# Two halves of the activations as one 512-column operand, with both sums added on VectorE

## The reference

```python
def chunk_relpos_attention(h, w_qkv, w_o, rel_bias):      # 16 heads of 64, chunks of 64 tokens
    q, k, v = split_heads(h, w_qkv)                       # h (256 x 1024) @ w_qkv (1024 x 3072)
    ...
        sc = jnp.einsum('bhqd,bhkd->bhqk', q_blk, k[:, :, k0:k1]).astype(jnp.float32) * scale
        sc = sc + bias[None, :, :, BAND - n_keys:]
        p = jax.nn.softmax(sc, axis=-1).astype(v.dtype)
    ...
    return merge_heads(o) @ w_o

def swiglu(h, w_gate, w_up, w_down):                      # 1024 -> 2816 -> 1024
    return (jax.nn.silu(h @ w_gate) * (h @ w_up)) @ w_down

def second_block(x, ...):
    h = rms_norm_2(x, g_pre_mix[i])
    m = chunk_relpos_attention(h, w_qkv[i], w_o[i], rel_bias[i // N_MIXERS])
    x = x + rms_norm_2(m, g_post_mix[i])
    h = rms_norm_2(x, g_pre_ffn[i])
    x = x + rms_norm_2(swiglu(h, w_gate[i], w_up[i], w_down[i]), g_post_ffn[i])
```

## Time and profile before

| | |
|---|---|
| median of 3 runs | 817.92 us (816.59 to 818.11) |
| the profiled execution's own time | 817.35 us |
| its span in the trace | 815.5 us |
| granted TensorE clock, mean | 0.978 of full speed |
| TensorE matmuls busy | 750.4 us (92%), 5438 matmuls |
| weight loads busy | 622.9 us (76%), 5438 |
| VectorE busy | 401.6 us (49%) |
| ScalarE busy | 332.6 us (41%) |
| DMA queue 1 | 67.2% of 16 engines' span |

### The profile page before, as it was taken

How to read it: one execution, slowest core, us unless ns; L and a number is a source line. 1 busy time by engine, 2 the same in 40 slices (tenths; PEclk the granted TensorE clock), 3 DMA queues, 4 the chain that set the end, 5 groups by cost and what they waited for, 6 DMA issues and landing times.

```text
span 815.5 us, 12982 instructions
## 1 busy us (share of the span) xinstructions
PE 750.4 (92%) x5438; PEld 622.9 (76%) x5438; DVE 401.6 (49%) x730; ACT 332.6 (41%) x597; POOL 23.8 (3%) x45
## 2 busy tenths in 40 slices
PE   8989999999999999996866868999998999999996
PEld 7888787888888885552443446999878999999995
DVE  5747755666758531110100108566657655565554
ACT  5476465455444331110110105556546444444442
POOL 1100000000000000000000002100002000000000
PEclk9999999999999999998989989999999999999998
DMA  9637365635987879999999999954343554556101
GB/s 337 208 130 197 138 220 191 221 131 168 380 322 254 344 315 423 420 420 421 420 421 422 420 401 354 364 201 155 121 139 126 184 200 162 194 170 204 53 1 52
DMA packets 83691, 203.99 MB, mean 250 GB/s; under 512 B 6960, under 2 KB 47536, under 8 KB 71088
## 3 DMA queue, kind: packets, MB, share of 16 engines
q1 hardware_dynamic: 83632, 203.15, 67.2%
HBM read 202.09 MB, written 1.05 MB: 249 GB/s over the span
## 4 chain that ended last, share of the span: by engine, by line
PE 77%; DMA 10%; DVE 4%; ACT 3%; issue 2%; SPq 1%; POOL 1%; DVEq 0%; ACTq 0%; POOLq 0%
PE ps L582 57%; DMA ext<-in_w_gate_e 7%; PE ps L863 5%; DMA big<-in_w_up_e 3%; PE ps L884 2%; PE ps L842 2%; PE ps L897 2%; DVE wl L1442 1%; SPq L451 1%; PE ps L945 1%; PE ps L563 1%; ACT junk L1097 1%; PE ps L959 1%; PE ps L973 1%; PE ps L760 1%
## 5 line engine op out<-in xcount | busy, mean ns | idle before, releaser
L1442 DVE TENSOR_TENSOR wl<-raw,wh 128x1024 fp32r<-128x1024 f32 (+3 forms) x180 | 213.5, 1200 | 138.6 <-ACT wh L1088 138.4
L1088 ACT CAST wh<-raw 128x1024 fp32r<-128x1024 f32 (+3 forms) x180 | 183.1, 1031 | 101.3 <-PE ps L582 101.2
L582 PE MATMUL ps<-fra,wh 128*128 128x256 f32 x1168 | 213.7, 285 | 5.9 <-DVE fra L1868 2.6
L582 PEld LDWEIGHTS ps<-fra,wh 128*128 128x128 f32 x1168 | 183.8, 193 | 8.3 <-DVE fra L1868 2.8
L582 PE MATMUL ps<-wh,fra 128*128 128x512 f32 (+3 forms) x668 | 188.8, 368 | 0.7 <-DVE gb L1654 0.4
L582 PE MATMUL ps<-fra,wl 128*128 128x256 f32 x584 | 166.0, 284 | 0.0
L582 PEld LDWEIGHTS ps<-wh,fra 128*128 128x128 f32 x668 | 118.9, 189 | 19.6 <-DVE wl L1442 1.5
L582 PE MATMUL ps<-wl,fra 128*128 128x512 f32 (+3 forms) x334 | 121.3, 363 | 0.0
L582 PEld LDWEIGHTS ps<-fra,wl 128*128 128x128 f32 x584 | 112.7, 193 | 0.0
L863 PE MATMUL ps<-ext,big 128*32 128x256 f32 x480 | 53.8, 446 | 23.0 <-DMA ext<-in_w_up_e 10.7
L582 PE MATMUL ps<-wh,frb 128*128 128x512 f32 x240 | 74.4, 391 | 0.0
(11 more groups left out here) (240 smaller groups left out, 809.8 us busy)
## 6 DMA issues: line engine op xcount, KB each, us to landing
ext<-in_w_up_e SPq DMA_DIRECT2D x23, 1024.0 KB, 26.1
raw<-in_w_in SPq DMA_DIRECT2D x16, 1024.0 KB, 5.1
raw<-in_w_gate_e SPq DMA_DIRECT2D x16, 1024.0 KB, 9.9
raw<-in_w_down_e SPq DMA_DIRECT2D x16, 1024.0 KB, 27.0
raw<-in_w_qkv SPq DMA_DIRECT2D x12, 1024.0 KB, 12.8
raw<-in_w_gate SPq DMA_DIRECT2D x11, 1024.0 KB, 5.2
raw<-in_w_up SPq DMA_DIRECT2D x11, 1024.0 KB, 5.1
raw<-in_w_down SPq DMA_DIRECT2D x11, 1024.0 KB, 4.9
```

The lines of the kernel that those rows point to most:

```text
L582: t = e.matmul(o, a, w, start=first and n == 0, stop=final and n == 2, skip_group_check=not check)
L1088: e.copy(halves(q)[0], piece_view(q)).then_inc(*up("wh", q))
L1442: e.tensor_tensor(l, piece_view(q), h.bitcast(F), ALU.subtract).then_inc(*up("wl", q))
```

## The change

The tile `fra` now holds, for each k, the upper half's 256 tokens and the lower half's 256 side by side, so that `hT_both[:, k]` is one operand of 512 columns. A new function `joint` replaces `features` for queries, keys, gate and up. For each (k, j) it issues one matmul of 512 columns (upper weights by both halves) into a whole bank, and one of 256 columns (lower weights by the upper half) into the left half of that bank. Each j has its own bank, so an output takes two banks. The left half and the right half of a bank are two sums that have to be added: `summed` on VectorE does it with a `tensor_reduce` over the two halves, one per bank, into the place in SBUF where the result goes. Then the scaling works on SBUF in place. The values of a quarter now share one bank, with their matmuls as before. The banks turn with the quarter (`quarter_banks`: queries c and c+1, keys c+2 and c+3, values c+4, modulo 4). Gate always uses banks 4 and 5, up always 6 and 7.

```diff
@@ -274,7 +274,8 @@
         wh, wl, fra, frb = (rounded.enter_context(nc.sbuf_tensor(n, s, FR)) for n, s in (
             ("wh", [P, PIECES, 1024]), ("wl", [P, PIECES, 1024]), ("fra", [P, 8192]), ("frb", [P, 4096])))
     ext = sb("ext", [P, EXT, 2048])
-    hT = [fra[:, a:a + 2048].rearrange("p (t n) -> p t n", t=8) for a in (0, 2048)]
+    hT = [fra[:, 0:4096].rearrange("p (t z n) -> p z t n", t=8, z=2)[:, z] for z in range(2)]
+    hT_both = fra[:, 0:4096].rearrange("p (t m) -> p t m", t=8)
     mT = [fra[:, a:a + 2048].rearrange("p (t n) -> p t n", t=8) for a in (4096, 6144)]
     ym = [frb[:, a:a + 1024].rearrange("p (t n) -> p t n", t=4) for a in (0, 1024)]
     mo = [fra[:, a:a + 2048].rearrange("p (t n) -> p t n", t=8) for a in (0, 2048)]
@@ -428,6 +429,10 @@
         b, half_ = FFN_AT[k]
         return bank[b][:, 256 * half_:256 * half_ + 256]
 
+    def quarter_banks(c):
+
+        return [(c + n) % 4 for n in range(5)]
+
     def causal_parts(s):
         return s[:, 0:128], s[:, 128:384]
 
@@ -630,6 +635,30 @@
                 t.then_inc(*up("piece", q))
                 yield
 
+        def joint(key, banks, freed, ready=(), later=(), row=None):
+
+
+            for q in wt.run[key]:
+                p = wt.pieces[q]
+                h, l = halves(q)
+                for point in ready if p.k0 == 0 else later if p.k0 == 4 else ():
+                    e.wait_ge(*point)
+                e.wait_ge(*at("wl", q))
+                for kk in range(p.rows):
+                    k = p.k0 + kk
+                    if row:
+                        e.wait_ge(*at(*row, k))
+                    for j, b in enumerate(banks):
+                        sl = slice(P * j, P * j + P)
+                        if k == 0:
+                            enter(b, *freed, j)
+                        e.matmul(bank[b][:, :], h[:, kk, sl], hT_both[:, k], start=(k == 0), stop=(k == 7),
+                                 skip_group_check=True)
+                        t = e.matmul(bank[b][:, 0:256], l[:, kk, sl], hT[0][:, k], start=False, stop=(k == 7),
+                                     skip_group_check=True)
+                t.then_inc(*up("piece", q))
+                yield
+
         def attention(name, heads, scores, columns, values):
 
             for step in range(heads + 3):
@@ -924,9 +953,23 @@
         def quarter(c):
 
             first = dict(ready=[at("lo", "pre", 0, 1)], later=[at("lo", "pre", 4, 1)]) if c == 0 else {}
-            yield from features(("q", c), 0, hT, ("kept q", c), **first)
-            yield from features(("k", c), 1, hT, ("kept k", c))
-            yield from tokens(("v", c), 1, hT, ("kept v2", c))
+            yield from joint(("q", c), quarter_banks(c)[0:2], ("summed q", c), **first)
+            yield from joint(("k", c), quarter_banks(c)[2:4], ("summed k", c))
+            b = quarter_banks(c)[4]
+            for q in wt.run["v", c]:
+                p = wt.pieces[q]
+                h, l = halves(q)
+                e.wait_ge(*at("wl", q))
+                if p.k0 == 0:
+                    enter(b, "kept v2", c, 1)
+                for kk in range(p.rows):
+                    for i in range(2):
+                        k, sl = p.k0 + kk, slice(P * i, P * i + P)
+                        t = two_term(bank[b][:, 256 * i:256 * i + 256],
+                                     ((hT[0][:, k, sl], h[:, kk]), (hT[1][:, k, sl], h[:, kk]), (hT[0][:, k, sl], l[:, kk])),
+                                     (k, i) == (0, 0), k == 7, check=False)
+                t.then_inc(*up("piece", q))
+                yield
 
         def other_quarters():
             for c in range(1, 4):
@@ -1034,8 +1077,8 @@
 
         for c in range(12):
             if c < 11:
-                whole(features(("fg", c), 4 + 2 * (c % 2), hT, ("scaled gate", c), row=("lo", "ffn") if c == 0 else None))
-                whole(features(("fu", c), 5 + 2 * (c % 2), hT, ("a", c)))
+                whole(joint(("fg", c), (4, 5), ("summed gate", c), row=("lo", "ffn") if c == 0 else None))
+                whole(joint(("fu", c), (6, 7), ("summed up", c)))
                 if c == 0:
                     spread("ffn row", 2)
             if c:
@@ -1342,7 +1385,8 @@
                 e.wait_ge(*at("piece", last["v", c]))
                 if (c, i) == (0, 0):
                     e.wait_ge(*at("factors"))
-                e.activation(H[:, i, 256 * c:256 * c + 256], bank[2 + i][:, 0:256], ACT.Copy, scale=rr[:, i:i + 1]).then_inc(
+                v = bank[quarter_banks(c)[4]][:, 256 * i:256 * i + 256]
+                e.activation(H[:, i, 256 * c:256 * c + 256], v, ACT.Copy, scale=rr[:, i:i + 1]).then_inc(
                     *up("kept v2", c, i))
 
         def other_quarters():
@@ -1881,23 +1925,38 @@
             e.tensor_copy(krow, bank[b][:, 0:256]).then_inc(*up(name, 0))
             e.wait_ge(*own())
 
+        def summed(name, c, q, dst, banks):
+
+            e.wait_ge(*at("piece", q))
+            for j, b in enumerate(banks):
+                e.tensor_reduce(dst[:, j, :], bank[b][:, :].rearrange("p (z n) -> p n z", z=2), AX, ALU.add).then_inc(
+                    *up("summed " + name, c, j))
+
+        def sum_q(c):
+            summed("q", c, last["q", c], qT[:, 2 * c:2 * c + 2, :], quarter_banks(c)[0:2])
+
+        def sum_k(c):
+            summed("k", c, last["k", c], kT[:, 2 * c:2 * c + 2, :], quarter_banks(c)[2:4])
+
+        rows = krow.unsqueeze(1).to_broadcast([P, 2, 256])
+
         def keep_q(c):
-            e.wait_ge(*at("piece", last["q", c]))
-            e.scalar_tensor_tensor(qT[:, 2 * c:2 * c + 2, :], bank[0][:, :].rearrange("p (j n) -> p j n", j=2), 0.125,
-                                   krow.unsqueeze(1).to_broadcast([P, 2, 256]), ALU.mult, ALU.mult).then_inc(
-                                       *up("kept q", c, 0))
+            v = qT[:, 2 * c:2 * c + 2, :]
+            e.wait_ge(*at("summed q", c, 1))
+            e.scalar_tensor_tensor(v, v, 0.125, rows, ALU.mult, ALU.mult).then_inc(*up("kept q", c, 0))
 
         def keep_k(c):
-            e.wait_ge(*at("piece", last["k", c]))
-            e.tensor_tensor(kT[:, 2 * c:2 * c + 2, :], bank[1][:, :].rearrange("p (j n) -> p j n", j=2),
-                            krow.unsqueeze(1).to_broadcast([P, 2, 256]), ALU.mult).then_inc(*up("kept k", c, 0))
+            v = kT[:, 2 * c:2 * c + 2, :]
+            e.wait_ge(*at("summed k", c, 1))
+            e.tensor_tensor(v, v, rows, ALU.mult).then_inc(*up("kept k", c, 0))
 
         def other_quarters():
             for c in range(1, 4):
                 yield from stream(("q", c))
-                for key, keep in (("k", keep_q), ("v", keep_k)):
+                for key, sums_, keep in (("k", sum_q, keep_q), ("v", sum_k, keep_k)):
                     pieces = stream((key, c))
                     yield next(pieces)
+                    sums_(c)
                     keep(c)
                     yield from pieces
 
@@ -1920,11 +1979,15 @@
             e.wait_ge(*at("factor", "fin", i))
             e.scalar_tensor_tensor(X[:, i, :], MO[:, i, :], rms("fin")[1][:, i:i + 1], gb[:, 1, :], ALU.mult,
                                    ALU.mult).then_inc(*up("block 1", i))
-        whole(stream(("k", 0)))
+        keys_ = stream(("k", 0))
+        next(keys_)
+        sum_q(0)
+        whole(keys_)
         e.wait_ge(*at("factors"))
         spread("krow", rr)
         vals = stream(("v", 0))
         next(vals)
+        sum_k(0)
         spread_row("krow", 6)
         keep_q(0)
         keep_k(0)
@@ -1963,13 +2026,15 @@
                                    ALU.mult, ALU.subtract).then_inc(*up("lo", "ffn", k))
         split_to(wt.run["o", 3][1] + AHEAD)
 
+        def two_of(v):
+            return v.rearrange("p (j n) -> p j n", j=2)
+
         def scaled_gate(c):
             if c:
                 e.wait_ge(*at("al", c - 1))
-            e.wait_ge(*at("piece", last["fg", c]))
-            e.tensor_tensor(S[0].rearrange("p (j n) -> p j n", j=2),
-                            bank[4 + 2 * (c % 2)][:, :].rearrange("p (j n) -> p j n", j=2),
-                            krow.unsqueeze(1).to_broadcast([P, 2, 256]), ALU.mult).then_inc(*up("scaled gate", c, 0))
+            summed("gate", c, last["fg", c], two_of(S[0]), (4, 5))
+            e.wait_ge(*own())
+            e.tensor_tensor(two_of(S[0]), two_of(S[0]), rows, ALU.mult).then_inc(*up("scaled gate", c, 0))
 
         for c in range(12):
             z = c % 2
@@ -1983,9 +2048,10 @@
                     spread("ffn row", rms("ffn")[1])
                     spread_row("ffn row", 2)
                     scaled_gate(c)
-                e.wait_ge(*at("piece", last["fu", c]))
+                summed("up", c, last["fu", c], two_of(S[1]), (6, 7))
+                e.wait_ge(*own())
                 e.wait_ge(*at("silu", c, 0))
-                e.tensor_tensor(S[1], S[0], bank[5 + 2 * z][:, :], ALU.mult).then_inc(*up("a", c, 0))
```

(1 more changed line is left out.)

## The result

The changed kernel takes 820.11 us (median of 8, 819.77 to 821.85) against 818.01 us for the kernel before, measured beside it (median of 8). The ratio is 1.0034, with a 95% interval of 1.0023 to 1.0045: slower, by about 2.8 us by the ratio and 2.1 by the medians. The profiled execution took 820.13 us with a span of 818.4, against 817.35 and 815.5 before.

A forecast was written before the change was run, and what follows sets the result against it. TensorE's own pace was taken as the bound, so savings and new waits count in full: +3.3 (quarters) - 4.5 + 1.7 + 0.1 = +0.6 on 817.35, 817.95; with the median 0.57 higher, 818.5 us, range 814 to 824.5.

The forecast's parts named there:

- likeliest case: Whole kernel: the forecast itself, kept at 0.55, own range 816 to 821, with 0.39 of it within 0.2%.
- the slow reduce: Quarters 1 to 3 and feed-forward start: reduce above 0.69 us; 822 at 0.95 us, 828 at 1.38; chance 0.17.
- the late queue: A late split makes TensorE wait within a piece: 2 to 4 us more, 821 to 823; chance 0.08.
- The reduce: VectorE's sum over a bank's two halves, 60 in all: 0.69 us alone, 1.3 us for a pair.
- Values of quarter 0: They wait for the first reduce to free bank 0: start at 512.85, 0.75 us later than before.
- Keys of quarter 1: Second block waits for bank 0 until quarter 0's values are copied out: starts at 526.9, 1.45 us later.
- Scores: At the ends of quarters 1 to 3, waiting for kept keys: 2.0 us later, then 0.65 more for each, 3.3 finally.
- the forecast wait of 0.95: Quarters 2 and 3: keys kept about 0.95 us after the time the scores used them before.
- Feed-forward: Joining saves 4.5 us; gate 1 waits 1.7 us for reduces between chunks 0 and 1, no other chunk waits.
- forecast saving of 6.1: TensorE, joined matmuls: 12.9 ns for each of 122 quarter and 352 feed-forward pairs, 1.6 + 4.5 us.
- the third rival: Joined matmuls: a pair takes 360 ns as before, the 6.1 us do not come, ends at 824.6; chance 0.07.
- its sign of being right: TensorE's joined matmuls: 512-column and 256-column matmuls 347 ns apart per pair; a pace of 357 ns would show it wrong.

The follow-up runs named there:

- the layout alone: Kernel before with only the two halves placed side by side for each k, matmuls of 256 columns, no reduce: 818.07 us, ratio 1.0003.
- widths in twos: Joint matmuls only in feed-forward chunks from 1 on, ordered two of 512 columns then two of 256; against the kernel before: 814.41 us, ratio 0.9954.

## Why the prediction was right

It forecast 818.5 with 814 to 824.5 and the largest chance, 0.44, on slower; 820.11 came. Its likeliest case was no change, at +0.6 us on the profiled execution, and +2.8 came. The mechanism stands, and the terms are below. The right side was in part luck. Of the 0.44 on slower, 0.32 belonged to three rivals, of which two fell (the slow reduce and the late queue) and the third came by half. And the distance of 1.6 us from the forecast is flattered: the changed kernel's median lies in the early group of its executions and the median before in the late one. Counted from the first matmul of the queries, less the 0.7 behind TensorE's last matmul, the change costs 3.3 us and not 0.6.

- **The reduce**, 0.69 us from two rows at a distance: 0.683 measured. The first rival (a slower reduce) fell with it.
- **Values of quarter 0**: start forecast at 512.85, measured 512.47. The wait was 1.7 us and not 1.1, because TensorE ran this quarter at 1.00 of its clock (0.54 between 499.0 and 502.7 before) and came earlier to the same reduce. Shift of the first scores: +0.44 against 0.75, but counted from the first matmul of the queries +0.91, and +1.74 against the layout alone, whose queries ran at full clock. It costs nothing, since the mask covers it, as forecast.
- **Keys of quarter 1**: wait for `keep_v` to 526.9, measured 526.46 and the start at 526.52.
- **Scores**: +2.0, +2.65, +3.3 forecast, +1.89, +2.84, +3.87 measured. The waits were 0.93, 1.12 and 1.12 by the trace. The first comes near because the mask was ready 0.39 earlier in this execution; the chain itself grew by 2.28. One reading was wrong: the 0.15 us between kept keys and scores was no slack. It is what passes between VectorE's end and TensorE's start where TensorE waits, too (540.23 to 540.37 here, 539.43 to 539.58 with the layout alone). That is 0.15 in each chain, and with it the forecast wait of 0.95 is 1.10, near the measured 1.12. The rest of the growth with each quarter, 0.14, is the saving, 0.17 us in three pieces and not 0.31.
- **Feed-forward**: the wait between chunks 0 and 1 was forecast at 1.7 and came at 1.6 (2.02 us from spread to gate against 0.44 before). The saving is the term that was mis-sized.

That term is "Two of 256 are 240.0 ns, so joining them saves 12.9 ns". It takes 227.1 ns for a 512-column matmul from a stretch where all neighbours have 512 columns. In turn with matmuls of 256 the pair takes 353 ns and not 347, which is 6 more on whichever of the two, and the joining saves 6.9. Over 352 pairs that is 2.1 us, over the 122 of the quarters 0.7, and the down blocks lose 0.03 us each, 0.3 together: 3.1 us of the forecast saving of 6.1. The sum by the measured terms, on TensorE's side: +3.87 at the end of the quarters, -0.15 in chunk 0 and what is ahead of it, +1.58 in the wait, 9 x -0.22 and -0.04 in gate and up, +0.3 in the down blocks is +3.58, which is the difference at TensorE's last matmul (811.38 against 807.80); these are differences of start times, so that they add up says nothing for the mechanism. The tail behind it was 0.7 us shorter, hence +2.9 in the spans. A sum that could have failed is the one of the quarters: waits of 1.66, 0.68, 0.93, 1.12 and 1.12 us, less the 0.66 that the layout alone has at step 4, less 0.84 saved, give 4.0 us. From the first matmul of the queries to the scores of step 12 the changed kernel takes 88.92 us and the layout alone 84.74, 4.2 more. The share of the saving that did not come is a smaller form of the third rival (a fixed cost that is not shed), on which the prediction had 0.07; its sign of being right was 347 ns a pair and its sign of being wrong 357, and 353 lies between them.

The Trainium skill's 2.5 ns ("TensorE: Matmul & The Clock Gate", "Back-to-back issue gap") stand there in a formula for an isolated matmul, not for a stream with its weight loads. That they would be the saving per pair is not borne out: 6.9 ns came, and with widths in twos 12.5.

## What to carry to other kernels

A pace belongs to a sequence, not to an instruction: before counting on a wider matmul's time, read it where its neighbours are the ones it will have, and group equal widths. An output that takes twice the banks and is added on another engine moves the release of those banks behind that engine's queue, so go through the queue at each place where a bank is reused or a result is needed at once; here six such places cost more than 480 matmuls saved, and moving one step ahead of a split got the loss back. A gap of 0.15 us between one engine's end and another's start is the passing on itself and no slack. And when two kernels differ by a microsecond, count in both traces from the first instruction that the change touches: first blocks that differed by 1.5 us hid two thirds of a gain of 2.1 us here.

## What the runs showed of the hardware

- fp32r matmuls of 512 and of 256 columns one by one take 353 ns a pair, two and two 347.5, where matmuls among their like take 227.1 and 120.0. A change of the PSUM bank costs nothing that shows (353 with either count of changes).
- A VectorE sum over two halves of a PSUM bank, 512 elements in and 256 out with a stride of 256 between the two terms, takes 683 ns, as much as a reduce of 512 elements to two outputs (690) or an instruction with 512 outputs (693).
- After three idle times of 3.5 us TensorE came back once at 0.50 of its clock and twice at full clock, falling soon behind (0.68 and 0.72 over 4 us); after 3.1 us it was at 0.51. After 2.57 us before the first queries it was at 0.54 in the trace of before and at 1.00 in that of after. After the new waits of the changed kernel, 1.7 us at most, it stayed at 1.00. Doubling some 1.28 us of VectorE work in eight places cost 17 us in all, 8 to 9 more than the waits by themselves.
- TensorE starts 0.14 to 0.15 us after the end of the VectorE instruction that it waits for (scores of step 4, with and without reduces).
